# Order of the softmax steps in the last attention of a two-block model: head by head on VectorE, exponentials ahead of one weight rounding, and three output panels open at the end

## The reference

```
def one_block(args):
    q_i, c_i, i = args
    s = jnp.einsum('bhqd,bhkd->bhqk', q_i, k, ...) * scale
    s = s + c_i[..., None] - c[:, :, None, :]
    s = jnp.where(kpos[None, :] <= qpos[:, None], s, -jnp.inf)
    p = jax.nn.softmax(s, axis=-1)
    return jnp.einsum('bhqk,bhkd->bhqd', p.astype(v.dtype), v)
...
o = forgetting_attention(q, k, v, c)
o = o * jax.nn.sigmoid(qg[..., d:])
x = x + o @ b_w_out[j]
```

## Time and profile before

| | us |
|---|---|
| median of 3 runs | 2096.43 (2096.16 to 2096.64) |
| the profiled execution | 2107.71 |
| its span | 2105.6, granted clock 0.992 |
| PE busy | 2068.7 (98%) |
| DVE, ACT, POOL busy | 969.1, 778.9, 853.6 |
| from the first pair's scores (1521.4) to `out3 + 3` (1714.75) | 193.3 |

### The profile page before, as it was taken

The page is one execution under the profiler, slowest core; times in us unless marked ns, Lnnn a source line. Parts: engine busy times, 40 slices in busy tenths (PEclk is TensorE's granted clock), DMA queues, the critical chain, the costliest instruction groups (busy, mean ns, idle before and its releaser), DMA issues.

```text
span 2105.6 us, 23893 instructions
## 1 busy us (share of the span) xinstructions
PE 2068.7 (98%) x9546; PEld 1688.0 (80%) x9546; DVE 969.1 (46%) x1457; ACT 778.9 (37%) x1112; POOL 853.6 (41%) x357
## 2 busy tenths in 40 slices
PE   9899999999999999999999999999998999999999
PEld 6788888878888888888788888887766678888887
DVE  6688778433322313434363351442456545425243
ACT  5445544634222214522422221254455543222222
POOL 3333433543444444434444444453322134444444
PEclk9999999999999999999999999999999999999999
DMA  4222222342323223323233222232211112323323
GB/s 170 73 71 81 79 81 71 110 153 81 100 92 100 98 93 97 100 90 101 90 100 101 91 96 94 100 115 76 90 51 51 40 61 92 109 91 99 102 90 110
DMA packets 55118, 194.27 MB, mean 92 GB/s; under 512 B 6112, under 2 KB 6368, under 8 KB 55008
## 3 DMA queue, kind: packets, MB, share of 16 engines
q1 hardware_dynamic: 55008, 192.75, 28.0%
HBM read 190.62 MB, written 2.10 MB: 92 GB/s over the span
## 4 chain that ended last, share of the span: by engine, by line
PE 92%; DVE 6%; ACT 1%; issue 1%; DMA 0%; POOL 0%; SPq 0%; DVEq 0%; POOLq 0%
PE ps L1251 28%; PE ps L1253 28%; PE ps L1252 28%; DVE arena L1190 2%; PE ps L1551 1%; PE ps L1357 1%; PE ps L1259 1%; PE ps L1560 1%; PE ps L1527 1%; DVE arena L891 0%; DVE arena L730 0%; DVE arena L719 0%; DVE a_lo L743 0%; PE ps L1343 0%; PE ps L1379 0%
## 5 line engine op out<-in xcount | busy, mean ns | idle before, releaser
L345 POOL TENSOR_TENSOR w_lo<-w_raw,w_hi 128x1024 fp32r<-128x1024 f32 x353 | 853.4, 2420 | 1240.0 <-ACT w_hi L362 1235.2
L1251 PE MATMUL ps<-a_hi,w_hi 128*128 128x512 f32 x1472 | 585.4, 398 | 9.8 <-DVE a_lo L748 3.7
L1253 PE MATMUL ps<-a_hi,w_lo 128*128 128x512 f32 x1472 | 575.6, 391 | 0.0
L1252 PE MATMUL ps<-a_lo,w_hi 128*128 128x512 f32 x1472 | 575.5, 391 | 0.0
L1251 PE MATMUL ps<-b_hi,w_hi 128*128 128x512 f32 x1240 | 489.3, 395 | 2.3 <-DVE b_lo L748 2.2
L362 ACT CAST w_hi<-w_raw 128x1024 fp32r<-128x1024 f32 x353 | 366.1, 1040 | 331.7 <-PE ps L1253 322.2
L1253 PE MATMUL ps<-b_hi,w_lo 128*128 128x512 f32 x1240 | 483.4, 390 | 0.0
L1252 PE MATMUL ps<-b_lo,w_hi 128*128 128x512 f32 x1240 | 482.9, 389 | 0.0
L719 DVE TENSOR_TENSOR arena<-ps,inv_rms 128x512 f32<-128x512 f32 x208 | 143.5, 690 | 487.4 <-PE ps L1253 467.7
L1251 PEld LDWEIGHTS ps<-a_hi,w_hi 128*128 128x128 f32 x1472 | 278.0, 189 | 71.9 <-issue 12.2
L1253 PEld LDWEIGHTS ps<-a_hi,w_lo 128*128 128x128 f32 x1472 | 277.7, 189 | 59.0
(11 more groups left out here) (177 smaller groups left out, 1519.0 us busy)
## 6 DMA issues: line engine op xcount, KB each, us to landing
w_raw<-in_panels SPq DMA_DIRECT2D x353, 512.0 KB, 3.4
x<-in_xT SPq DMA_DIRECT2D x16, 256.0 KB, 2.7
outT<-x SPq DMA_DIRECT2D x8, 256.0 KB, 2.4
consts<-in_const SPq DMA_DIRECT2D x1, 528.5 KB, 8.4
arena<-in_rows SPq DMA_DIRECT2D x1, 256.0 KB, 4.5
arena<-in_ws SPq DMA_DIRECT2D x1, 256.0 KB, 4.8
consts<-in_late SPq DMA_DIRECT2D x1, 168.0 KB, 2.6
params<-in_param SPq DMA_DIRECT2D x1, 116.0 KB, 2.0
```

Of the source, the lines that this page charges most:

```text
L345: nc.gpsimd.tensor_tensor(w_lo[:, p % RING, :], w_raw[:, p % RING, :], w_hi[:, p % RING, :].bitcast(F), ALU.subtract).then_inc(w_low, 1)
L1251: nc.tensor.matmul(o, wh, hi[:, kt, :], start=(kt == 0), stop=False)
L1252: nc.tensor.matmul(o, wh, lo[:, kt, :], start=False, stop=False)
L1253: ins = nc.tensor.matmul(o, wl, hi[:, kt, :], start=False, stop=(kt == tiles - 1))
```

## The change

DVE and ACT go through the softmax side by side: first the four blocks of side 0, then those of side 1. `scale_prob` is cut in two, each with a reciprocal of four sums and four scalings: side 0's stand before the query's `scale_out`, side 1's behind it. The `low_hid` of a pair moves from its end to the next pair, behind the maxima (and stays at the end in the last call). On ACT `softmax(a)` goes ahead of `high(p + 2)`. In the last call a third panel, `out3 + 2`, gets bank 6 and is started before its two predecessors are complete.

```diff
         def bank_of(p):
+            if p == S["out3"] + 2:
+                return 6
             return p if p < GROUPS else p % 2
...
-        SOFTMAX_ORDER = [(0, 3), (1, 3), (0, 2), (0, 0), (1, 2), (1, 0), (0, 1), (1, 1)]
-        SCORES_BEFORE = (1, 2, 5, 5, 6, 6, 7, 8)
-        MAXIMA_BEFORE = (1, 2, 4, 4, 6, 6, 7, 8)
+        SOFTMAX_ORDER = [(side, b) for side in (0, 1) for b in (3, 2, 0, 1)]
+        SCORES_BEFORE = (1, 5, 5, 7, 7, 7, 7, 8)
+        MAXIMA_BEFORE = (1, 3, 3, 4, 5, 7, 7, 8)
...
             def pair(m, a):
                 p = S["qg"] + 2 * m if m is not None else None
+                if a is not None:
+                    softmax(a)
                 if m is not None:
                     high(p + FEED)
-                if a is not None:
-                    softmax(a)
-                if m is not None:
                     act.wait_ge(evicted, p + 1)
...
-            def scale_prob(a):
-                dve.wait_ge(exped, a * 2 * BLK + 2 * BLK)
-                link(v.reciprocal(row_inv[:, :], row_sum[:, :]))
-                for side in range(2):
-                    for b in range(BLK):
...
+            def scale_prob(a, side):
+                dve.wait_ge(exped, a * 2 * BLK + (side + 1) * BLK)
+                of = slice(side * BLK, (side + 1) * BLK)
+                link(v.reciprocal(row_inv[:, of], row_sum[:, of]))
+                for b in range(BLK):
...
                 if a is not None:
                     maxima(a)
+                    if a > 0:
+                        low_hid(a + HID_ATTN, a - 1, o_all[:, :], B)
+                    scale_prob(a, 0)
                 if m is not None:
                     scale_out(q_raw[:, :], p).then_inc(evicted, 1)
                 if a is not None:
-                    scale_prob(a)
+                    scale_prob(a, 1)
                     copy_prob(a)
...
-                    if a > 0:
-                        dve.wait_ge(hid_high, HID_ATTN + a)
...
-                if a is not None:
+                if m is None:
                     low_hid(a + (HID_ATTN + 1), a, o_all[:, :], B)
...
-                    if p >= GROUPS:
+                    if p >= GROUPS and p != S["out3"] + 2:
                         pe.wait_ge(evicted, p - 1)
...
-                    product(S["out3"] + 1, b_hi, b_lo, part=(0, 3))
+                    product(S["out3"] + 1, b_hi, b_lo, part=(0, 6))
                 if a is not None:
                     turn_prob(a)
                 if m is not None:
                     product(p + 1, a_hi, a_lo, part=(4, DT))
                 else:
-                    product(S["out3"] + 1, b_hi, b_lo, part=(3, 7))
+                    product(S["out3"] + 1, b_hi, b_lo, part=(6, 7))
+                    pe.wait_ge(copied_odd, a * 2 + 2)
+                    product(S["out3"] + 2, b_hi, b_lo, part=(0, 3))
                 if a is not None:
                     if m is not None:
                         pe.wait_ge(sums_read, m + (R_Q + 1))
                     attend(a)
+                if m is None:
+                    product(S["out3"] + 2, b_hi, b_lo, part=(3, 7))
...
             product(S["out3"] + 1, b_hi, b_lo, part=(7, DT))
-            linear(S["out3"] + 2, DT - 2, b_hi, b_lo, None, None)
+            product(S["out3"] + 2, b_hi, b_lo, part=(7, DT))
+            linear(S["out3"] + 3, DT - 3, b_hi, b_lo, None, None)
```

More of the change, by code:

```diff
@@ L266, in build @@
             "q_squared", "q_normed", "gate_log", "gate_arg", "gate_done"))
+        S = START
         def bank_of(p):
+            if p == S["out3"] + 2:
+                return 6
             return p if p < GROUPS else p % 2
@@ L284, in build @@
         block = ctx.enter_context(nc.Block())
-        S = START
         SCORES = {(0, 3): (2, 0), (0, 2): (3, 0), (0, 0): (3, 384), (0, 1): (4, 0),
@@ L665, in pair @@
                 p = S["qg"] + 2 * m if m is not None else None
-                if m is not None:
-                    high(p + FEED)
                 if a is not None:
@@ L670, in pair @@
                 if m is not None:
+                    high(p + FEED)
                     act.wait_ge(evicted, p + 1)
@@ L1182, in maxima @@
                                     AX.X, ALU.max, negate=True).then_inc(maxed, 1)
-            def scale_prob(a):
-                dve.wait_ge(exped, a * 2 * BLK + 2 * BLK)
-                link(v.reciprocal(row_inv[:, :], row_sum[:, :]))
-                for side in range(2):
-                    for b in range(BLK):
-                        at = prob[side][:, OFF_P[b]:OFF_P[b] + P * (b + 1)]
-                        v.tensor_scalar(at, at, row_inv[:, side * BLK + b:side * BLK + b + 1], None,
-                                        ALU.mult).then_inc(scaled, 1)
+            def scale_prob(a, side):
[3 more added lines that the diff above has]
+                for b in range(BLK):
+                    at = prob[side][:, OFF_P[b]:OFF_P[b] + P * (b + 1)]
+                    v.tensor_scalar(at, at, row_inv[:, side * BLK + b:side * BLK + b + 1], None,
+                                    ALU.mult).then_inc(scaled, 1)
             def copy_prob(a):
```

## The result

The changed kernel takes 2086.1 us (median of 10 runs, 2084.1 to 2089.4) against 2098.2 us for the kernel before (10 runs, 2094.7 to 2108.1). The ratio is 0.9929 (95% interval 0.9912 to 0.9945): 0.7% faster, about 15 us, where 16.8 were forecast. A repetition with 6 runs gave 2086.7 and 0.9924. The two medians alone are 12 us apart; the kernel before scatters over 13 us, the changed one over 5. The time itself lies 6.5 us above the forecast of 2079.6 and inside its range, for a reason given in the part on why the prediction was right.

The account below looks back on a forecast made before the run. PE bounds the kernel, through idle ahead of the transposes and its lower clock. Pairs 11.3 + 6.7 = 18.0 us, less 1.2 in the last call, give 16.8: 2096.4 - 16.8 = 2079.6 us, range 2073 to 2090.

Parts of the forecast that it names:

- What holds the scalings: In the pairs: whatever VectorE scales while POOL subtracts is held until POOL ends; one scaling took 2.51 us.
- The pairs: Seven query-and-score pairs: six lose 1.89 us of idle each, 11.3 us; with the clock part 18.0 us.
- T 8.2: Time in us from a pair's first score matmul; POOL's first run was forecast from 8.2 to 10.6.
- The overlap of the transposes with the sums: In each pair, transposes starting before the sums end: at most 0.15 us more gain.
- The first pair: First of the seven pairs: maxima start 1.9 us later, scalings are held by POOL's second run; gain nothing.
- The term 4 x 1.67: Transposes in four later pairs: 1.67 us each regained where TensorE fell to its lower clock, 6.7 us in all.
- I take the gain over unchanged: Whole kernel: the gain worked out from the profiled execution, 16.8 us, is subtracted unscaled from the median of 2096.4.
- the first rival: Pairs: the idle goes but the clock part doesn't; gain 10.1 us, time 2086.3; chance 0.13.
- The last call: Last call and panels behind: 0.3 us won, a new 4.1 us wait, 1.5 us lower clock; net 1.2 us lost.
- The fourth scaling is held: Side 1's fourth scaling waits for POOL's second run; a pair gains 0.4 us, time 2094.8; chance 0.14.

Follow-up runs that it names:

- the open panels alone: The kernel before with only the three open panels of the last call added, pairs unchanged: 2103.2 us, ratio 1.001 to the kernel before.
- ACT's order back: The changed kernel with high(p + 2) put back ahead of the exponentials on ACT: 2083.1 us, ratio 0.9923 to the kernel before.
- both halves behind the eviction: The changed kernel with both halves of the scalings behind the query's eviction: 2112.5 us, ratio 1.0044 to the kernel before.
- `low_hid` back: The changed kernel with low_hid back at the end of its pair, ahead of the maxima: 2102.6 us, ratio 1.0006 to the kernel before.
- the one with four steps: The changed kernel with ACT's order back and four steps of out3 + 2, all behind attend, in the last call: 2082.1 us, ratio 0.9901 to before.
- the kernel with the pairs alone: The changed kernel with its last call put back to two open panels: 2082.9 us, ratio 0.9921 to the kernel before.

## Why the prediction was right, and where it was off

- **What holds the scalings: shown.** The step rested on one row of 2.51 us. Moving POOL's run alone (one line) gave as much as the whole change; moving the maxima alone took it away.
- **The pairs: right, one term too small.** T 8.2 for POOL's first run was 8.30, its end 10.6 was 10.70, the first maximum 1.5 was 1.52, 20.3 us between pairs were 20.11. The overlap of the transposes with the sums was put at 0.15 at most and left out of the sum; it is there in each of the six pairs, and each is 0.2 shorter than forecast. Six pairs: 6 x (22.22 - 20.11) = 12.7 instead of 11.3.
- **The first pair: right**, 1.88 us left; POOL's two runs stand 0.17 us apart there.
- **The clock in the pairs: right for the profile, wrong for the time it was taken from.** The term 4 x 1.67 came from one execution of the kernel before. In the changed kernel's profile no pair fell, so the five falls make 8.35 there. One of the five is luck: the first pair's idle is still 1.88 us, and its fall went all the same. The step that was off is "I take the gain over unchanged": the four falls were subtracted from a median of three runs, 2096.4, that can't have held them all. For 51 further runs of the kernel before the mean granted clock is known: the 13 below 2097 us show 0.998 or more, the 18 above 2106 show 0.990 to 0.993, and the profiled execution of 2107.7 shows 0.992. An estimate from that: a clock of 0.998 over 2095 us means some 8 us at half clock, 4 us lost in the whole program, which is room for two or three falls of 1.67 and nothing else; 0.992 means four times as much. So where the execution had few falls, the change gave back mostly idle time: 12.7 for the pairs, less 1.3 to 2.2 for the open panels, gives 2085 to 2086, and 2086.1 was measured. That is also the number of the first rival, 2086.3. Its mechanism, that the falls stay when the idle goes, is not what the profile shows; the number came out through the base. That the time still lies in the range is in part luck, since the range was widened for that rival and for one more or less fall, not for a base without falls.
- **How much it scatters.** Runs of the kernel before lay from 2094.0 to 2110.8 us, 61 in all, with a median of 2101.7, and seven falls are 11.7 us. The slower a run, the lower its clock, so the clock carries nearly all of that scatter; in which stretch it fell, only the profiles show: five, and in the kernel with only the open panels one, of seven pairs. The 16.8 us are a mean over a quantity that a single profile doesn't fix.
- **The transposes at full clock.** The Trainium skill ("TensorE: Matmul & The Clock Gate", "Part 4: PE-mode transpose") has full clock not engaging for transposes; here they ran 2.35 us at a granted clock of 1.00 pair after pair, so this support for the first rival fell.
- **The last call: right to 0.1 us.** 4.06 us of wait (4.1 forecast), 29.04 us to `out3 + 3` (29.1). The lower clock behind it was taken as 1.5 us, from the row behind 2.24 us of idle, with twice that as the bound. It was 2.6 in the first profile, which makes the open panels a loss of 2.2 us there, and 1.5 to 1.7 in the five other profiles with the same last call (the repetition, the open panels alone, ACT's order back, both halves behind the eviction, `low_hid` back), by the time from the start of `out3 + 3` to the last matmul, 387.3 us in the kernel before. So the size was right as a rule, and one execution differed from it.
- **One slip in a rival's sum.** "The fourth scaling is held" counts 2.8 us, 0.4 for seven pairs, though the first pair gains nothing; for six it is 2.4, and the time 2095.2.
- **Left open:** 1.15 us more between the last matmul and the end of the span than in the profile of the kernel before. In the repetition of the changed kernel it is 0.45 more, so part of it changes from run to run; nothing was tried on it.

The sum with the measured terms: 12.7 + 8.35 - 2.2 = 18.85 for the profile, against 16.8.

## What to carry to other kernels

Where two engines lock each other out, the order on one can be right and the time still wrong: look at the start of the held instruction against the start of the other engine's, and move the cheaper of the two. Here one moved line on ACT gave as much as a reordered softmax. Look also at what the moved run meets in its new place. And before a gain read from one profile is subtracted from a median, compare the granted clocks of the two: a cost that comes and goes may be in one and not in the other. Opening another PSUM panel covers one wait by taking away the work that covered the next; count how many matmuls stand behind the release of the oldest buffer before taking them ahead.

## What the runs showed of the hardware

The clock's fall depends on more than the idle ahead of it, but was never absent behind 4 us. Granted clock in the 10 us from PE's restart, in the profiles of these kernels: 0.69 to 0.86 in all seven with 4.00 to 4.06 us of idle; 1.00 in all three with 2.04 or less; behind 2.24 us it fell in the kernel before and not in the two others. Ahead of the transposes, 1.89 us of idle brought it in five, one and three of seven pairs of three kernels (before, open panels alone, `low_hid` back), and 2.30 us in five of six. One row each, of the changed kernel repeated, of the one with four steps and of the kernel with the pairs alone:

```profile
1691.16:1701.16 10.00, 10.00 (x37) 8.09 (x38) 7.15 (x8) 4.25 (x7) 4.88 (x2) 0.83 0.39 112
```

```profile
1687.05:1697.05 10.00, 10.00 (x44) 8.26 (x45) 8.60 (x8) 4.54 (x7) 6.05 (x3) 1.00 0.37 113
```

```profile
1681.49:1691.49 10.00, 9.82 (x42) 7.87 (x43) 7.42 (x7) 4.37 (x6) 4.97 (x2) 1.00 0.15 54
```

Held were DVE instructions with one SBUF input (scalings, a copy) and with two (line 1210, 746). Not held was the eviction of a PSUM bank with one SBUF operand: line 719 never took over 0.693 us in 224 instances of the kernel before, and in the changed kernel's pair above it starts inside POOL's run (1632.12, POOL from 1631.02 to 1633.42) and takes 0.69; the reciprocal of four sums behind it, 1632.73, takes 0.17. The Trainium skill ("SBUF — State Buffer", "SBUF: two separate sides") counts VectorE instructions with two SBUF inputs, and those that run in a two-port mode, as the ones that take the lock. The held rows with two inputs agree; in which mode the scalings and the reciprocal ran, no run here shows.
